# Feed-forward up and gate computed as 2x2 block products in seven split products a pair, ahead of all down products

## The reference, cut to what matters

```python
D_FF = 2816
def conv_ffn(h, w_up, conv_w, conv_b, w_down):
    up, gv = jnp.split(h @ w_up, 2, axis=-1)          # (1024 x 1024) @ (1024 x 5632)
    up = causal_dwconv(up, conv_w, conv_b)            # 3 taps along the tokens
    return (jax.nn.gelu(up) * gv) @ w_down            # (1024 x 2816) @ (2816 x 1024)

    # in second_block, after the mixers:
    x = x + jnp.concatenate([y_gla, y_s5, y_rg], axis=-1) @ w_out[l]
    h = rmsnorm(x, mlp_norm[l])
    x = x + conv_ffn(h, w_up[l], mlp_conv_w[l], mlp_conv_b[l], w_down[l])
    return rmsnorm(x, final_norm)
```

## Time and profile before

| | us |
|---|---|
| median of three runs | 2325.5 |
| profiled execution, its span | 2323.7 |
| median less span (launch and end, outside the span) | 1.8 |
| TensorE (PE) busy in the span | 2158.1 (93%) |
| DVE / ACT / POOL busy | 1130.5 / 531.2 / 945.7 |

### The profile page before, as it was taken

How to read it: one execution, slowest core, us unless ns; L and a number is a source line. 1 busy time by engine, 2 the same in 40 slices (tenths; PEclk the granted TensorE clock), 3 DMA queues, 4 the chain that set the end, 5 groups by cost and what they waited for, 6 DMA issues and landing times.

```text
span 2323.7 us, 26206 instructions
## 1 busy us (share of the span) xinstructions
PE 2158.1 (93%) x10096; PEld 1692.4 (73%) x10096; DVE 1130.5 (49%) x1787; ACT 531.2 (23%) x900; POOL 945.7 (41%) x579
## 2 busy tenths in 40 slices
PE   6999999988967999995998997999999999999997
PEld 5888889987835666653765566688888888888875
DVE  7998335664131222225888776744331332233135
ACT  4110057666221111112310034212110110011011
POOL 3553346751736567003038821243323323323324
PEclk9999999999987999997999998999999999999998
DMA  5553165654466787227222211211111111111113
GB/s 218 210 216 126 45 167 156 179 168 145 159 255 239 293 311 293 105 105 274 91 91 83 99 55 39 89 55 46 46 41 59 46 46 46 55 50 41 56 29 116
DMA packets 79104, 286.93 MB, mean 123 GB/s; under 512 B 24152, under 2 KB 24408, under 8 KB 71320
## 3 DMA queue, kind: packets, MB, share of 16 engines
q1 hardware_dynamic: 43720, 185.17, 23.1%
q10 hardware_dynamic: 27712, 61.48, 7.6%
q0 software_dynamic: 7552, 38.60, 4.6%
HBM read 212.28 MB, written 80.81 MB: 126 GB/s over the span
## 4 chain that ended last, share of the span: by engine, by line
PE 63%; DVE 9%; issue 3%; POOL 3%; ACT 2%; DMA 2%; DVEq 0%; SPq 0%; ACTq 0%; POOLq 0%
PE ps L1004 12%; PE ps L1006 12%; PE ps L1008 12%; PE ps L1258 4%; PE ps L1242 2%; PE ps L1238 2%; PE ps L1240 2%; PE ps L1239 2%; PE ps L1162 1%; PE ps L1226 1%; PE ps L986 1%; PE ps L989 1%; PE ps L988 1%; PE ps L1102 1%; PE ps L1365 1%
## 5 line engine op out<-in xcount | busy, mean ns | idle before, releaser
L1004 PE MATMUL ps<-work_part 128*128 128x512 f32 x1760 | 548.8, 393 | 9.9 <-POOL work_part L777 7.4
L1008 PE MATMUL ps<-work_part 128*128 128x512 f32 x1760 | 543.2, 390 | 0.0
L773 POOL CAST work_part<-ring 128x1024 fp32r<-128x1024 f32 (+2 forms) x124 | 121.9, 983 | 739.2 <-PE ps L1008 614.3
L1004 PEld LDWEIGHTS ps<-work_part 128*128 128x128 f32 x1760 | 330.6, 188 | 84.3 <-POOL work_part L777 7.5
L1008 PEld LDWEIGHTS ps<-work_part 128*128 128x128 f32 x1760 | 331.3, 188 | 69.2
L1006 PE MATMUL ps<-work_part 128*128 128x512 f32 x1152 | 354.7, 389 | 0.0
L777 POOL TENSOR_TENSOR work_part<-ring,work_part 128x1024 fp32r<-128x1024 f32 (+2 forms) x124 | 284.1, 2291 | 15.9 <-PE ps L1456 6.1
L1006 PEld LDWEIGHTS ps<-work_part 128*128 128x128 f32 x1152 | 216.3, 188 | 44.9
L1006 PE MATMUL ps<-hT_part,work_part 128*128 128x512 f32 x608 | 188.8, 392 | 0.0
L2283 DVE TENSOR_TENSOR hT<-ps,hT 128x1024 f32<-128x1024 f32 x40 | 49.0, 1225 | 261.5 <-PE ps L1008 245.0
L1006 PEld LDWEIGHTS ps<-hT_part,work_part 128*128 128x128 f32 x608 | 115.0, 189 | 24.3
(11 more groups left out here) (398 smaller groups left out, 3378.5 us busy)
## 6 DMA issues: line engine op xcount, KB each, us to landing
pages<-w_moe SPq DMA_DIRECT2D x16, 2048.0 KB, 9.9
ring<-w_up_units SPq DMA_DIRECT2D x44, 512.0 KB, 3.4
w_parts<-work_part SPq DMA_DIRECT2D x36, 512.0 KB, 3.6
work_part<-w_parts SPq DMA_DIRECT2D x36, 512.0 KB, 4.1
pages<-w_moe SPq DMA_DIRECT2D x16, 1024.0 KB, 6.7
x_slots<-zeros ACTq DMA_DIRECT2D x31, 512.0 KB, 4.0
work<-x_slots ACTq DMA_DIRECT2D x31, 512.0 KB, 5.8
y_slots<-work ACTq DMA_DIRECT2D x31, 512.0 KB, 2.7
```

What stands on the lines that cost most here:

```text
L773: pool.tensor_copy(WHI[n % 2][:, 0:cols], w).then_inc(whi_ready, 1)
L1004: pe.matmul(ps[:, c], whi[:, w], hi[k][:, c], start=(k == 0), stop=False)
L1008: mm = pe.matmul(ps[:, c], wlo[:, w], hi[k][:, c], start=False, stop=(k == len(hi) - 1))
```

## The change

The change computes up and gate of a pair together. The pair's weights are seen as a 2x2 block matrix (rows: up, gate; columns: the first and the second four contraction tiles), the activations as another (rows: the same halves of the contraction; columns: the two token halves). The 2x2 product is made of seven block products instead of eight (Winograd's form of Strassen's method). Each block product has 4 x 3 = 12 matmuls of 128x512.

- Weights a11, a12 (up), a21, a22 (gate) give the sums s1 = a21 + a22, s2 = s1 - a11, s3 = a11 - a21, s4 = a12 - s2. POOL makes the four sums (`pair_combine`) and seven low parts (`pair_low`), ACT the seven high parts (`pair_high`).
- The activations' blocks and sums (`XV`: a0, t1, b0, b1, t2, t3, t4) are made once, at the start.
- PSUM holds three half-bank sums a pair, twice over. Between products that add into the same place, ACT copies the intermediate sum out (`copy_p1`, `copy_p5`, `copy_u2`), and DVE adds them (`up_first`, `up_second`, `up_gate`).
- All 22 pairs run ahead of all down units. The products go to DRAM (`y_keep`) and come back by group; the residual `h` is parked in DRAM too (`h_keep`) and comes back after the pairs. The groups of the down units are now 3, 6, 6 and 7 pairs.

The core of the diff:

```diff
-FF_GROUPS = [range(0, 6), range(6, 12), range(12, 18), range(18, FF)]
-FF_KEEP = 7
+FF_GROUPS = [range(0, 3), range(3, 9), range(9, 15), range(15, FF)]
+FF_MOST = 7
+        PRODUCTS = [("P1", 0), ("P5", 0), ("P2", 0), ("P6", 0), ("P3", 0), ("P7", 0)]
+        for _j in range(1, FF):
+            PRODUCTS += [("P1", _j), ("P4", _j - 1), ("P2", _j), ("P5", _j), ("P6", _j), ("P3", _j), ("P7", _j)]
+        PRODUCTS.append(("P4", FF - 1))
             # SP
+            def load_pair(j):
+                sem_, was = pair_loaded[j % 2]
+                for i in range(2):
...
+                    if j >= 2:
+                        sp.wait_ge(products_done, product_count["P4", j - 2])
+                    sp.dma_start(raw(PAIR_R[j % 2][i]), w_up[2 * j + i]).then_inc(sem_, 16)
+            def save_y(j):
+                sp.wait_ge(prod_ready, j + 1)
+                sp.dma_start(y_keep[j], YUP[j % 2]).then_inc(y_saved[j % 2][0], 16)
+                for j in range(2, FF):
+                    load_pair(j)
+                    save_y(j - 2)
+                if u == U_DOWN + RING:
+                    save_y(FF - 2)
+                    bring_h()
+                    save_y(FF - 1)
             # POOL
+            def pair_combine(j):
...
+                pool.tensor_tensor(s3, a11, a21, ALU.subtract).then_inc(pair_sums[0], 1)
+                pool.tensor_tensor(s1, a21, a22, ALU.add).then_inc(pair_sums[0], 1)
+                pool.tensor_tensor(s2, s1, a11, ALU.subtract).then_inc(pair_sums[0], 1)
+                pool.tensor_tensor(s4, a12, s2, ALU.subtract).then_inc(pair_sums[0], 1)
+            for j in range(1, FF):
+                pair_combine(j)
+                for v in LO_ORDER:
+                    pair_low(j, v)
             # PE
+            def product(name, j, w, x, to, first, joined):
+                bank_ = PAIR_PS[j % 2][to]
+                pe.wait_ge(*past(pair_lo, 7 * j + LO_ORDER.index(w) + 1))
+                for k in range(4):
+                    pe.matmul(bank_, whi[:, cols], xhi, ...)
+                    pe.matmul(bank_, whi[:, cols], xlo, ...)
+                    mm = pe.matmul(bank_, wlo[:, cols], xhi, ...)
+                mm.then_inc(products_done, 1)
+             # ACT
             for j in range(FF):
...
+                if j >= 1:
+                    copy_p1(j)
+                    if j + 1 < FF:
+                        for v in HI_ORDER[:3]:
+                            pair_high(j + 1, v)
+                    copy_p5(j)
+                    if j + 1 < FF:
+                        for v in HI_ORDER[3:5]:
+                            pair_high(j + 1, v)
...
+                    copy_u2(j)
+                    if j + 1 < FF:
+                        for v in HI_ORDER[5:]:
+                            pair_high(j + 1, v)
...
+                up_affine(j)
+                up_gelu(j)
             # DVE
+            for j in range(1, FF):
+                up_first(j)
...
+                up_scale(j, 0)
+                up_second(j)
+                up_scale(j, 1)
+                if j == FF - 1:
+                    for f in FF_GROUPS[0]:
+                        f_low(f)
+                up_gate(j)
+                up_conv(j)
+                up_product(j)
```

More of the change, by code:

```diff
@@ L461, in build @@
         MIX_LO = [Wr[29 + h][:, :] for h in range(4)] + [Wr[t][:, :] for t in range(4)]
[L462 to L477, removed]
+        n_mlp = add_late_norm(Hp, "mlp_norm", Wp[22:25], take(1), take(1), None)
+        P_DOWN = {g: take(8) for g in range(3)}
+        def part(t):
+            return Wr[t][:, :] if t >= 0 else hTr[t + NT][:, :]
+        def raw(t):
+            return Hp[t + NT] if t < 0 else W[:, t, :] if t < 37 else ring[:, t - 37, :]
@@ new lines, in w_of @@
+        def w_of(v, j):
+            r, i, h, q = WV[v]
+            return second(part(PAIR_H[j % 2][h]), q), second(part(PAIR_R[j % 2][r]), i), second(raw(PAIR_R[j % 2][r]), i)
+        P5_COPY = [second(raw(PAIR_R[i][3]), 1) for i in range(2)]
+        U2_COPY = [second(raw(PAIR_H[i][3]), 1) for i in range(2)]
+        UP, YUP = [raw(-8), raw(-7)], [raw(-6), raw(-5)]
+        GATE = [second(raw(-4), i) for i in range(2)]
+        b0_ = bank(P_DOWN[0])
+        PAIR_PS = [(PS[b0_][:, 0:HALF], PS[b0_][:, HALF:S], PS[(b0_ + 1) % SLOTS][:, 0:HALF]),
+                   (PS[(b0_ + 2) % SLOTS][:, 0:HALF], PS[(b0_ + 2) % SLOTS][:, HALF:S], PS[(b0_ + 3) % SLOTS][:, 0:HALF])]
@@ L1883, in _, with copy_p1, copy_p5 @@
             norm_std(n_mlp)
+            for k in range(4):
+                x_high_turn("t3", k)
+            def copy_p1(j):
+                act.wait_ge(products_done, product_count["P1", j])
+                act.activation(second(UP[j % 2], 0), PAIR_PS[j % 2][0], ACT.Copy).then_inc(up_parts[0], 1)
+            def copy_p5(j):
+                act.wait_ge(products_done, product_count["P5", j])
+                act.activation(P5_COPY[j % 2], PAIR_PS[j % 2][2], ACT.Copy).then_inc(up_parts[0], 1)
@@ new lines, in _ @@
+            for m in range(8):
+                dve.wait_ge(mm_done, done(P_OUT2 + m))
+                dve.tensor_tensor(Hp[m], PS[bank(P_OUT2 + m)][:, :], Hp[m], ALU.add).then_inc(h_ready, 1)
+                if m < 7:
+                    dve.wait_ge(h_ready, 8 + m + 1)
+                if m >= 2:
+                    norm_add(n_mlp, m - 1)
+                if 1 <= m <= 4:
+                    x_turn_1(m - 1)
+                if 2 <= m <= 5:
+                    x_low("t1", m - 2)
+                if 4 <= m <= 6:
+                    x_turn_234(m - 4)
@@ L2720, in final_add @@
+            for i in range(3):
+                for m in range(8):
+                    dve.wait_ge(mm_done, done(P_DOWN[i] + m))
+                    if i == 0 and m % 2 == 0:
+                        dve.wait_ge(*past(h_back[m // 2], 16))
+                    dve.tensor_tensor(Hf[m], PS[bank(P_DOWN[i] + m)][:, :], Hf[m], ALU.add).then_inc(h_ready, 1)
+                    if 1 <= m <= len(FF_GROUPS[i + 1]):
+                        f_low(FF_GROUPS[i + 1][m - 1])
             def final_add(half, t):
```

443 lines of the change are left out of this document (351 added, 92 removed).

## The result

| | before | after |
|---|---|---|
| time, median (range) of 4 runs | 2325.9 us (2324.95 to 2327.72) | 2292.7 us (2290.54 to 2294.53) |
| ratio, 95% interval | | 0.9854 (0.9839 to 0.9868) |
| profiled span | 2323.7 us | 2291.2 us |

A forecast was written before the change was run, and what follows sets the result against it. TensorE was taken to bound the feed-forward, so each matmul removed saves 0.2267 us. From 2325.5 us: less 59.8, plus 5 (pairs), 11 (start) and 4 (end) gives 2285.7, forecast 2286 us, range 2269 to 2311.

The forecast's parts named there:

- What goes: Feed-forward pairs: 96 matmuls become 84 in each of 22 pairs, at 0.2267 us each, 59.8 us less.
- Rival E: Block products: matmuls into one half-bank run slower than 0.2267 us; 0.24 takes back 24 us, 2310 us; chance 0.04.
- The steady pair: Each pair after the first: 19.04 us of matmuls plus 0.25 us of waiting, 5 us in all, bounds 0 and 25.
- cover (b): In each pair, product P7 waits for ACT's copy of the second sum, behind s1's and s2's high parts; slack 0.2 to 0.5 us.
- Rival A: Pairs: DVE and POOL exclude each other for full operations and become the bound, 20.9 us a pair, 2320 us; chance 0.15.
- The loads: Each pair's two 512 KB loads: second issued 0.36 us later, landing 4.2 us after that; 4.7 us taken in all.
- cover (a): In each pair, product P3 waits for ACT's copy of P5, behind high parts that wait for the load; slack 0.5 us.
- rivals B: Pairs: the two loads land after 5.5 to 6 us, 10 to 20 us more, 2296 to 2303 us; chance 0.15.
- C: Pairs: the second load lands after 7.5 us, delaying ACT's copy of P5 by 2.8 us a pair; 2340 us, slower; chance 0.04.
- The end: First down tiles: late low parts cost 1 us, unit 4's load behind the return of h 3; 4 us, bounds 0 and 10.
- The start: First two pairs: waits for DVE, ACT and POOL around the norm cost 11 us, bounds 5 and 18.
- Some hold-ups: At the start, unsized delays added to DVE's 7.6 us before product P2(0), which was to end at 8.5 to 9.5 us.

The follow-up runs named there:

- actorder: The changed kernel with ACT's copy of the second sum moved ahead of the next pair's high parts of s1 and s2; 2289.2 us, ratio 0.9816.
- eighth: The changed kernel with product P2 of every pair run twice into the same place; 2345.6 us, ratio 1.0064 to the kernel before the change.
- notaps: The changed kernel without one convolution tap and the second scaling of every pair, the other tap 32 columns wide; 2293.9 us in one run.
- end: The changed kernel with down units 4 and 5 loaded ahead of the return of h and the last two products' stores; 2292.2 us, ratio 0.9833.
- apart: The changed kernel with POOL starting pair 1's weight sums only after DVE has made the eight low parts of t3 and t4; 2290.0 us, one run.
- fill: The changed kernel with 54 extra, unused matmuls placed in TensorE's waits of the first two pairs; 2289.5 us, ratio 0.9835.
- early: The changed kernel with DVE's low parts of t3, t4 and ACT's high parts of t4 ahead of the wait for the norm's root; 2283.8 us, ratio 0.9809.

## Why the prediction came out as it did

The direction, the mechanism and the range held (2292.7 in 2269 to 2311). That the total came so near is luck in part: the start was 13.4 us over its term, and four smaller things gave 6.1 back (the pairs 1.2, the end 1.7, the waits of before 2.3, and 0.9 by which the part ahead ended earlier). By its steps:

- **What goes, 59.8 us.** Right. 264 matmuls less; 0.2267 us each (actorder, eighth). Rival E is out.
- **The steady pair, +0.25 each.** Right: 0.18. The cause is cover (b), shown by actorder. POOL's computed 19.1 us in 19.04 came out as 305.4 / 330 x 19.22 = 17.8: its 190 operations took 1.61 us in the mean, where the sum had 19.1 / 11 = 1.74. Rival A's 20.9 us did not come.
- **The loads.** Nearly right: a pair's second load landed 4.6 us after its issue in the median and 5.6 at most, against 4.2 assumed. That is 4.9 from the first issue, where the sum had 4.7, and within cover (a)'s slack of 0.5, so rivals B and C are out for this kernel. C's 7.5 us was not met in the pairs. B's own price was added up wrongly: 10 to 20 us more than 2286 is 2296 to 2306, not 2303. Its mechanism is real, as notaps shows.
- **The end, +4.** 2.3 at the first down units, by the mechanism named (end), the tail's 5.0 as before. The wait of 1.8 us near the end, of which 0.3 is left, was not in the sum. Nor was the one of 0.8 at the start, where the prediction says that there was no wait before.
- **The start, +11, bounds 5 to 18.** Wrong in size: 24.4, beyond its upper bound. This is the step that failed, and more than all of the miss of 7 us.

The start's own times, from P1(0)'s first matmul (forecast as the prediction counts them, measured from the timelines of after, 1576.60 taken off):

| | forecast | measured |
|---|---|---|
| norm's sum done | 11.5 | 16.2 |
| P6(0) begins | 15 | 19.1 |
| P6(0) ends | 17.8 | 24.4 |
| RB copied | 20.1 | 27.6 |
| P7(0) ends | 25.5 | 36.1 |
| P4(0) begins | 31 | 44.4 |

Two prices explain it. DVE's operations were put at "some 0.7", the price alone, though the exclusion had been read from the earlier trace rows and charged to the steady pair; POOL works through most of the start too. The eight low parts of t3 and t4 are 8 us of the 13.4 by which the last row is late (13.6 us against 5.6; apart shows the cause). The earlier ones, 1.7 us for each of tile 3's three turns and 2.31 instead of 1.22 for the square sum behind them, lie ahead of the norm's sum and make some 4 us. The other is the clock, which the forecast did not speak of: 3.54 for 1.84 in the sum, 5.28 for 2.72 in P6(0) (1595.72 to 1601.00), 4.92 for 2.72 in P4(0) (1621.00 to 1625.92), 6.5 us in sum, of which fill brought back 5.2. With the eight low parts the forecast's 11 would have been 19, with fill's 5.2 as well 24. That this meets 24.4 is partly luck: the 4 us ahead of the norm's sum are not in it, and from RB's copy to P4(0) only 5.9 us more passed than forecast (16.8 for 10.9), not 8. "Some hold-ups" stood in the prediction as words, with no number.

One thing was computed right in an unhelpful way: the prediction followed DVE's list (the root's copy, the scaling, then the low parts) without asking whether the low parts need the root. They don't, and early's 10.3 us come from that.

## What to carry to other kernels

An exclusion or a price that is measured once must be charged in every stretch where both engines work; the start of a phase, where all helpers build at once, is where it costs, and the steady state may hide it entirely. Count a wait of TensorE twice if several follow each other: once as itself and once as the clock after it, and look at whether matmuls without use can lie in it. Transfers that do not meet today meet when an engine becomes faster: look at what its product's store will then lie on. Here, where a product was taken out of a loop of 22, most of the price was paid at the loop's start, so look there first for list entries that stand behind a wait that they don't need.

## What the hardware showed that was not expected

- **The clock falls in short waits.** After waits of 2.69 and 1.36 us with three matmuls between them the granted clock was 0.50, and the norm's sum took 1.92 times its length; before, with one wait of 0.84 us here, it was 1.00 throughout. It was back at 1.00 after P6(0), 0.50 again around the wait of 5.32 us, and 1.00 in all of these stretches with matmuls in the waits (fill).
- **DVE's scalar_tensor_tensor with two SBUF inputs is excluded as tensor_tensor is.** 1.7 us for 512 columns beside POOL (6.78 for four), where three of the same line alone took 2.07.
- **A fuller helper did not hurt, an emptier one did not help.** With POOL busy for 93% of the pairs TensorE lost 0.18 us a pair, and nothing in actorder; taking 120 us of DVE's work away made the pair 0.37 us longer, and the traces show a store on top of each load there (second load 5.4 us instead of 4.6, store 6.2 instead of 2.6).
